# Hybrid streaming encoder step: the eight tiles of squares of a norm are added on GpSimd, and TensorE multiplies one tile by the averaging matrix

## The chip, the cores and the metric

The kernel runs on one core of one Trainium2 chip. The metric is the device time of one execution in microseconds; the number given for a kernel is the median of several executions. The engines are called by the names of the profile: PE (TensorE), ACT (ScalarE), DVE (VectorE), POOL (GpSimd) and SP (the queue of the transfers).

## The reference

Two layers of an encoder trunk work on 1024 prompt frames and 32 sample frames of width 1024, all in float32. Each layer normalizes its stream four times: before and after the mixer, and before and after the MLP.

```
def rms_norm(x, g):
    xf = x.astype(jnp.float32)
    r = lax.rsqrt(jnp.mean(xf * xf, axis=-1, keepdims=True) + EPS)
    return (xf * r).astype(x.dtype) * g
...
h = rms_norm(xp, g_pre_mix[l]) * (1 + sc1) + sh1
... two head groups of attention on project(h, w_in[l]) give o ...
xp = xp + gt1 * rms_norm(jnp.dot(o, w_out[l]), g_post_mix[l])
# mlp_sublayer
h = rms_norm(x, g_pre) * (1 + scale) + shift
u = jnp.square(jax.nn.relu(jnp.dot(h, w_up)))
return x + gate * rms_norm(jnp.dot(u, w_down), g_post)
```

The mean runs over the 1024 features of a frame. The change is about this mean alone.

## The kernel before

The activations lie transposed: features on the 128 partitions, in `KT` = 8 feature tiles, and the 1056 frames along the free dimension, cut into `NCH` = 3 chunks of `CH` = 352 frames. Products are formed from float32 operands that are split into a high and a low part (`hh`, `hl`, `wh`, `wl`, `uh`, `ul`), three matmuls for each product (lines 1522 to 1524).

A norm of one chunk passes over four engines. ACT squares all eight tiles of the chunk in one instruction into `sq` (`pre_sq`, line 611, and `post_sq`, line 630) and raises `sq_ok`. PE multiplies the eight tiles of `sq` by `onesd`, a 128x128 matrix filled with 1/1024, and accumulates them in one PSUM bank (`mean`, line 1552), so that every partition holds the mean of its frame. ACT turns the mean into the reciprocal root `rb` with a logarithm and an exponential (`norm_rb`, lines 603 and 605). DVE scales by it: `pre_scale` (line 1056) and `pre_lo` (line 1072) for a norm ahead of a projection, where ACT writes `hh` between the two (`pre_hi`, line 620); `post_rms` (line 1081) and `post_add` (line 1091) for a norm that goes back into the stream.

The four norms of a layer are called `NPRE1`, `NPOST1`, `NPRE2` and `NPOST2`. With three chunks and two layers there are 24 means. Every engine has its instructions in an order that is written out by hand, and each executes them strictly in that order; `npos` numbers the 24 means in this order. Around the entry to the MLP PE has this order: the groups `y` 0 to 11 of the output projection's second half (24 matmuls each, `q` is the group's number), with the mean of `NPOST1` chunk 0 behind group 4, of `NPRE2` chunk 0 behind group 7, of `NPOST1` chunk 1 behind group 8, and of `NPRE2` chunk 1 and `NPOST1` chunk 2 behind group 11; then the MLP's first step, with the mean of `NPRE2` chunk 2 behind its fourth group. Below these six are called m1 to m6. The same six stand, with `NPOST2` and the next layer's `NPRE1`, around the boundary between the two layers, behind shorter groups of 12 matmuls (1.9 us each). In the last step of the last layer there are three `NPOST2` means, the third of them at the very end.

The squares of a `NPRE` norm are those of the stream that the `NPOST` norm of the same chunk has just written. So a chain leads from m1 through ACT, DVE (`post_rms`, `post_add`), ACT (`pre_sq`) to m2, and from m2 through `pre_scale`, `pre_lo`, `post_rms` and `post_add` of the next chunk on DVE to the squares of m4.

POOL has only memsets, and copies and subtractions in the attention stage (lines 510 to 561); between these stages it is idle.

Of the kernel before, what the change touches and what calls it, by code (L numbers as in the profile page):

```python
# [15 lines left out]
ALU = mybir.AluOpType  # L16
# [8 lines left out]
KT = D // P  # L25
SEQ, NEW = 1024, 32
TOK = SEQ + NEW
NCH = 3
CH = TOK // NCH
# [3 lines left out]
DEPTH = 2  # L33
# [27 lines left out]
NPRE1, NPOST1, NPRE2, NPOST2 = range(4)  # L61
# [11 lines left out]
def build(nc, a):  # L73
    ctx = ExitStack()
    with ctx:
        base = 16512

        def at(name, shape, dt, off):
            return nc.alloc_sbuf_tensor_at(name, shape, dt, offset=base + off)

        def sem(name):
            return ctx.enter_context(nc.semaphore(name))
# [5 lines left out]
        sq = at("sq", [P, KT, TOK], F32, 0)  # L88
# [71 lines left out]
        def small(name, shape, dt):  # L160
            n = int(np.prod(shape[1:])) * (2 if dt == BF16 else 4)
            t = nc.alloc_sbuf_tensor_at(name, shape, dt, offset=base + cpos[0])
            cpos[0] += (n + 31) // 32 * 32
            assert base + cpos[0] <= 229344, (name, cpos[0])
            return t

        ident = small("ident", [P, P], F32)
        onesd = small("onesd", [P, P], F32)
# [39 lines left out]
        ps = nc.alloc_psum_tensor("ps", [P, 8, 512], F32)  # L208
# [11 lines left out]
        def sm(name):  # L220
            if name not in S:
                S[name] = sem(name)
            return S[name]

        def wait_apart(e, held, *waits):

            for name, v in (held, *waits):
                if isinstance(v, int):  # L230
                    if v > 0:
                        e.wait_ge(sm(name), v)
                else:
                    e.wait_ge(sm(name), v)
# [34 lines left out]
        def n_of(it):  # L269

            return it[1] if it[0] == "f" else N_FM + it[1]
# [16 lines left out]
        def npos(l, nu, c):  # L288

            if nu == NPRE1:  # L290
                return c if l == 0 else 12 * l - 2 + 2 * c
            if nu == NPOST2:
                return 12 * l + 9 + (2 * c if l + 1 < DEPTH else c)
            return 12 * l + 3 + 2 * c + (nu == NPRE2)

        def slot(l, n):

            return (l * NW + n) % 2
# [209 lines left out]
        @block.gpsimd  # L508
        def _(pool):
            pool.memset(scp[:, :, :], 0.0).then_inc(sm("scp_zero"), 1)  # L510
            pool.memset(zerob[:, :], 0.0).then_inc(sm("zero_ok"), 1)
            pool.memset(epst[:, :], EPS).then_inc(sm("eps_ok"), 1)
            for l in range(DEPTH):

                wait_apart(pool, ("zero_ok", 1), ("w_used", l * NW + W_WO0))
                pool.memset(svh[:, :, 64:128].bitcast(F32), 0.0).then_inc(sm("sz_ok"), 1)
                pool.memset(svl[:, :, 64:128].bitcast(F32), 0.0).then_inc(sm("sz_ok"), 1)

                wait_apart(pool, ("zero_ok", 1), ("so_lo", (l + 1) * 16))
                pool.memset(fvh[:, :, 64:128].bitcast(F32), 0.0)  # L520
                pool.memset(fvl[:, :, 64:128].bitcast(F32), 0.0).then_inc(sm("fz_ok"), 1)
                n = 1
                for h in range(2):
                    for stack, value in ((k2, 1.0), (q2, -1.0)):

                        wait_apart(pool, ("zero_ok", 1), ("fz_ok", l * 5 + n))
                        pool.memset(stack[h][64:68, :].bitcast(F32), value).then_inc(sm("fz_ok"), 1)
                        n += 1

                def stacks_own(t, h):  # L530

                    pr = l * 4 + t
                    r = slice(64 * h, 64 * h + 64)
                    if t or h:
                        pool.wait_ge(sm("fs_mm"), pr * 16 if h else pr * 16 - 8)
                    else:
                        pool.wait_ge(sm("so_lo"), (l + 1) * 16)
                    pool.tensor_copy(q1[h][r, :], qf[r, t, 0:SEQ]).then_inc(sm("fq_own"), 1)
                    if h == 0:
                        pool.tensor_copy(q2[h][r, :], qf[r, t, 0:SEQ]).then_inc(sm("fq_own"), 1)  # L540
                    pool.tensor_copy(k1[h][r, :], kf[r, t, 0:SEQ]).then_inc(sm("fq_own"), 1)

                def o_lo(t, b):

                    c0 = (512, 0)[b]
                    pool.wait_ge(sm("fo_hi"), (l * 4 + t) * 2 + b + 1)
                    pool.tensor_tensor(hl[:, t + 4, c0:c0 + 512], qf[:, t, c0:c0 + 512], hh[:, t + 4, c0:c0 + 512].bitcast(F32),
                                       ALU.subtract).then_inc(sm("fo_lo"), 1)

                stacks_own(0, 0)  # L550
                for t in range(4):
                    pool.wait_ge(sm("fz_ok"), 5 * (l + 1))
                    pool.wait_ge(sm("fo_lo"), l * 8 + max(0, 2 * t - 1))
                    stacks_own(t, 1)
                    pool.wait_ge(sm("fq_own"), l * 20 + 5 * t + 5)
                    if t:
                        o_lo(t - 1, 1)
                    if t < 3:
                        stacks_own(t + 1, 0)
                    o_lo(t, 0)  # L560
                o_lo(3, 1)


        @block.scalar
# [954 lines left out]
        def _(pe):  # L1519
            def three(out, w_hi, w_lo, m_hi, m_lo, k, nk, start=True, stop=True):  # L1520

                pe.matmul(out, w_hi, m_hi, start=start and k == 0, stop=False)  # L1522
                pe.matmul(out, w_hi, m_lo, start=False, stop=False)  # L1523
                return pe.matmul(out, w_lo, m_hi, start=False, stop=stop and k == nk - 1)  # L1524
# [4 lines left out]
            for i in range(TT + 1):  # L1529
                pe.wait_ge(sm(f"xrow_in{i % 8}"), 16 * (i // 8 + 1))  # L1530
                w = P if i < TT else NEW
                for hf in range(2):
# [3 lines left out]
                    for k in range(4):  # L1536
                        ins = pe.transpose(ps[:, q % 4, k * w:(k + 1) * w], xrow[i % 8][0:w, (4 * hf + k) * P:(4 * hf + k + 1) * P], ident[0:w, 0:w])
# [7 lines left out]
            def mean(l, nu, c):  # L1545

                idx = npos(l, nu, c)
                s = idx % 2
                pe.wait_ge(sm("sq_ok"), idx + 1)
                pe.wait_ge(sm("ln_ok"), max(0, idx - 1))  # L1550
                for k in range(KT):
                    ins = pe.matmul(ps[:, 4 + s, 0:CH], onesd[:, :], sq[:, k, c * CH:(c + 1) * CH], start=(k == 0), stop=(k == KT - 1))  # L1552
                ins.then_inc(sm("mean_ok"), 1)

            def modulate(out, halves):
# [8 lines left out]
            def mod_columns(out, rows):  # L1564

                pick = ident[:, :].rearrange("p (g n) -> p g n", g=4)[:, :, 0:2]
                return pe.matmul(out, rows, pick, start=True, stop=True, skip_group_check=True)

            for l in range(DEPTH):

                pe.wait_ge(sm("zero_ok"), 1)
                if l == 0:
# [9 lines left out]
                    for b in range(NB1):  # L1582
                        ins = mod_columns(ps[:, 6, 8 * b:8 * b + 8], mrow1[:, b * P:(b + 1) * P])
# [36 lines left out]
                for q, it in enumerate(PJ):  # L1620
                    b, n = q % 4, n_of(it)
# [12 lines left out]
                    if it[0] == "t":  # L1634
                        _, u, i = it
# [3 lines left out]
                        for k in range(KT):  # L1639
                            ins = three(ps[:, b, 0:w], hh[:, k, ts], hl[:, k, ts], whv[:, k, :], wlv[:, k, :], k, KT)  # L1640
                    else:
                        _, blk, j, c = it
                        cs = slice(c * CH, (c + 1) * CH)
                        if blk < 2:
                            pe.wait_ge(sm("h_ok"), l * 6 + c + 1)
                        for k in range(KT):
                            ins = three(ps[:, b, 0:CH], whv[:, k, j * P:(j + 1) * P], wlv[:, k, j * P:(j + 1) * P],
                                        hh[:, k, cs], hl[:, k, cs], k, KT)
# [173 lines left out]
                for b in range(NB2):  # L1822
                    ins = mod_columns(ps[:, 7, 8 * b:8 * b + 8], mrow[:, b * P:(b + 1) * P])
# [25 lines left out]
                for w in range(4):  # L1849
# [5 lines left out]
                    for hd in range(4):  # L1855
# [4 lines left out]
                        if w < 2:  # L1860
                            ins = pe.matmul(out, qn, kst[r, w, :], start=True, stop=True)
# [5 lines left out]
                        ins = pe.matmul(out[:, PAST:W], identb[0:NEW, 0:NEW], causb[0:NEW, 0:NEW], start=False, stop=True)  # L1867
                    ins.then_inc(sm("a_mm"), 1)
                for w in range(4):
# [4 lines left out]
                    for kb, c0 in enumerate(starts):  # L1874
                        ins = pe.transpose(ps[:, (2, 6)[w % 2], kb * P:(kb + 1) * P], ap[w][:, c0:c0 + P], ident[:, :])
# [3 lines left out]
                    for hd in range(4):  # L1879
# [3 lines left out]
                        if w < 2:  # L1883
                            pe.matmul(out, cvs[:, 64 * w:64 * w + 64], pt[:, 0, pc], start=True, stop=False)
                            ins = pe.matmul(out, vs_new[NEWP:P, 64 * w:64 * w + 64], pt[NEWP:P, 1, pc], start=False, stop=True)
                        else:
                            for kb in range(2):
                                pe.matmul(out, cvf[:, kb, h * HD:(h + 1) * HD], pt[:, kb, pc], start=(kb == 0), stop=False)
                            ins = pe.matmul(out, vf[NEWP:P, TT, h * HD:(h + 1) * HD], pt[NEWP:P, 2, pc], start=False, stop=True)
# [13 lines left out]
                for r in range(2):  # L1903
                    n0 = l * NW + W_WO0 + r * 2
                    for q in range(12):

                        b, j, c = (q // 6, (q // 3) % 2, q % 3) if r == 0 else ((q // 2) % 2, q % 2, q // 4)
# [3 lines left out]
                        for k in range(KT):  # L1911
                            ins = step(W_WO0 + b, ps[:, q % 4, 0:CH], b, j, slice(c * CH, (c + 1) * CH), k, KT, hh, hl)
# [86 lines left out]
            for i in range(TT + 1):  # L1999
                t0 = i * P if i < TT else TAIL  # L2000
                pe.wait_ge(sm("x_ready"), DEPTH * 6 + 1 + (t0 + P - 1) // CH)
                for hf in range(2):
# [3 lines left out]
                    for k in range(4):  # L2006
                        ins = pe.transpose(ps[:, q % 4, k * P:(k + 1) * P], xr[:, 4 * hf + k, t0:t0 + P], ident[:, :])  # L2007
# [63 lines left out]
```

## Time and profile before

| what | us |
|---|---|
| median of 3 runs | 3165.98 |
| lowest and highest of them | 3157.59 and 3182.37 |
| profiled execution, its own time | 3182.45 |
| its span, first to last instruction | 3180.7 |
| PE busy in it | 2973.7 |
| POOL busy in it | 82.9 |
| mean granted clock of PE, as a share of full speed | 0.938 |

The profile comes from one execution, which took 16.5 us more than the median of the three. Busy times of the engines lie beside each other; PE, with 93% of the span, is the one that is hardly ever idle.

### The profile page before, as it was taken

What the parts mean: (1) busy time and instruction counts of PE and PEld (TensorE: products, weight loads), DVE (VectorE), ACT (ScalarE), POOL (GpSimd) and SP (SyncE); (2) the same over time, 40 slices, a digit from 0 to 9 for tenths busy, and PEclk for the clock granted to TensorE, in tenths of its full rate; (3) what the DMA queues carried; (4) which work ended last, traced back from release to release, by engine and by line L of the source; (5) the groups of instructions that cost most, each with busy time, mean ns of one, the idle gap of its engine ahead of it and who ended that gap; (6) DMA issues with size and microseconds to landing.
All of it is one profiled execution on the core that took longest, in us unless ns stands there. A gap on an engine that the chain in (4) does not pass through costs nothing. (4 is left out here: it accounts for less than half of the span.)

```text
span 3180.7 us, 48146 instructions
## 1 busy us (share of the span) xinstructions
PE 2973.7 (93%) x19659; PEld 2757.7 (87%) x19675; DVE 1316.5 (41%) x2391; ACT 964.9 (30%) x1944; POOL 82.9 (3%) x79
## 2 busy tenths in 40 slices
PE   6998878889999999999999988788999999999998
PEld 5998657759899999999989966677699999999997
DVE  4114647721633333333361356476136333333334
ACT  5212436622511122111242144365133211111222
POOL 0000011100000000000000000111000000000000
PEclk8998679969999999999999978799699999999998
DMA  7111230013221111112211113101212111111121
GB/s 279 41 57 56 80 107 2 17 40 109 81 67 64 56 53 49 56 53 66 106 65 54 43 55 133 54 2 43 88 57 72 51 43 41 51 40 53 40 81 55
DMA packets 135345, 203.33 MB, mean 64 GB/s; under 512 B 8352, under 2 KB 90320, under 8 KB 134672
## 3 DMA queue, kind: packets, MB, share of 16 engines
q1 hardware_dynamic: 135200, 201.27, 18.4%
q8 instruction: 106, 1.74, 0.2%
q14 instruction: 39, 0.32, 0.0%
HBM read 170.45 MB, written 31.00 MB: 63 GB/s over the span
## 5 line engine op out<-in xcount | busy, mean ns | idle before, releaser
L1522 PE MATMUL ps<-hh,wh 128*128 128x352 f32 x2304 | 755.3, 328 | 13.7 <-DVE wl L1045 11.0
L1524 PE MATMUL ps<-hh,wl 128*128 128x352 f32 x2304 | 743.8, 323 | 0.0
L1523 PE MATMUL ps<-hl,wh 128*128 128x352 f32 x2304 | 742.3, 322 | 0.0
L1522 PE MATMUL ps<-uh,wh 128*128 128x352 f32 x1536 | 500.2, 326 | 4.1 <-DVE modn L1472 2.6
L1523 PE MATMUL ps<-ul,wh 128*128 128x352 f32 x1536 | 493.0, 321 | 0.0
L1524 PE MATMUL ps<-uh,wl 128*128 128x352 f32 x1536 | 492.9, 321 | 0.0
L1522 PEld LDWEIGHTS ps<-hh,wh 128*128 128x128 f32 x2304 | 435.2, 189 | 18.9 <-DVE wl L1045 11.0
L1523 PEld LDWEIGHTS ps<-hl,wh 128*128 128x128 f32 x2304 | 436.7, 190 | 1.3
L1524 PEld LDWEIGHTS ps<-hh,wl 128*128 128x128 f32 x2304 | 435.1, 189 | 0.0
L1045 DVE TENSOR_TENSOR wl<-raw,wh 128x2048 fp32r<-128x2048 f32 (+1 forms) x90 | 206.2, 2291 | 370.5 <-ACT wh L567 370.5
L567 ACT ACTIVATE wh<-raw 128x2048 fp32r<-128x2048 f32 (+1 forms) x90 | 172.0, 1911 | 580.8 <-PE ps L1899 580.8
L1485 DVE TENSOR_TENSOR y<-ps,y 128x352 f32<-128x352 f32 x336 | 173.3, 523 | 363.6 <-PE ps L1524 363.3
L1522 PEld LDWEIGHTS ps<-uh,wh 128*128 128x128 f32 x1536 | 288.7, 188 | 6.7 <-DVE ul L1451 4.0
L1523 PEld LDWEIGHTS ps<-ul,wh 128*128 128x128 f32 x1536 | 288.9, 188 | 0.5
L1524 PEld LDWEIGHTS ps<-uh,wl 128*128 128x128 f32 x1536 | 288.1, 188 | 0.0
L1446 DVE TENSOR_TENSOR u_t<-r_t 128x352 f32<-128x352 f32 x192 | 100.8, 525 | 436.6 <-ACT r_t L973 434.5
L973 ACT ACTIVATE r_t<-ps 128x352 f32<-128x352 f32 x192 | 89.0, 464 | 515.6 <-PE ps L1524 515.6
L1522 PE MATMUL ps<-wh,hh 128*128 128x256 f32 (+1 forms) x720 | 208.5, 290 | 0.0
L1523 PE MATMUL ps<-wl,hh 128*128 128x256 f32 (+1 forms) x720 | 204.2, 284 | 0.0
L1524 PE MATMUL ps<-wh,hl 128*128 128x256 f32 (+1 forms) x720 | 203.3, 282 | 0.0
L1522 PEld LDWEIGHTS ps<-wh,hh 128*128 128x128 f32 x720 | 136.5, 190 | 0.4 <-issue 0.4
L1524 PEld LDWEIGHTS ps<-wh,hl 128*128 128x128 f32 x720 | 136.8, 190 | 0.0
(250 smaller groups left out, 3960.4 us busy)
## 6 DMA issues: line engine op xcount, KB each, us to landing
ada_v<-w_ada SPq DMA_DIRECT2D x32, 1024.0 KB, 6.9
raw<-w_up SPq DMA_DIRECT2D x32, 1024.0 KB, 5.1
raw<-w_down SPq DMA_DIRECT2D x32, 1024.0 KB, 4.9
raw<-w_in SPq DMA_DIRECT2D x16, 1024.0 KB, 5.6
x_kept<-xr SPq DMA_DIRECT2D x6, 1408.0 KB, 9.4
xf<-x_kept SPq DMA_DIRECT2D x2, 4224.0 KB, 12.7
x_kept<-xf SPq DMA_DIRECT2D x6, 1408.0 KB, 5.5
xr<-x_kept SPq DMA_DIRECT2D x2, 4224.0 KB, 13.1
```

The source lines that it names most:

```text
L567: return act.activation(out, in_, ACT.Copy, **kw)
L973: act.activation(r_t[q % 2][:, :], ps[:, q % 4, 0:CH], ACT.Relu).then_inc(sm("u_relu"), 1)
L1045: dve.tensor_tensor(wl[slot(l, n)][:, 0:w], raw[slot(l, n)][:, 0:w], wh[slot(l, n)][:, 0:w].bitcast(F32), ALU.subtract).then_inc(sm("w_lo" ...
L1446: dve.tensor_tensor(u_t[q % 2][:, :], r_t[q % 2][:, :], r_t[q % 2][:, :], ALU.mult).then_inc(sm("u_sq"), 1)
L1485: dve.tensor_tensor(y[:, kt, cs], ps[:, DB[last][q], 0:CH], y[:, kt, cs], ALU.add).then_inc(sm("d_add"), 1)
L1522: pe.matmul(out, w_hi, m_hi, start=start and k == 0, stop=False)
L1523: pe.matmul(out, w_hi, m_lo, start=False, stop=False)
L1524: return pe.matmul(out, w_lo, m_hi, start=False, stop=stop and k == nk - 1)
```

## The change

For 20 of the 24 means POOL adds the eight tiles of squares in place by halves: four tiles to four, two to two, one to one, three instructions one behind the other. PE then multiplies only tile 0 of `sq` by the averaging matrix. PE waits for `sum_ok` from POOL where it waited for `sq_ok` from ACT. The function `summed` leaves four means as they were: the three of `NPRE1` in the first layer, and the last of all (`NPOST2`, chunk 2, last layer). POOL's new work stands behind its attention work of each layer, in the order of the means. Nothing changes on ACT and DVE.

```diff
+        def summed(l, nu, c):
+            if (l == 0 and nu == NPRE1) or (l + 1 == DEPTH and nu == NPOST2 and c == 2):
+                return None
+            return npos(l, nu, c) - NCH
...
+            def sum_squares(l, nu, c):
+                cs = slice(c * CH, (c + 1) * CH)
+                i = summed(l, nu, c)
+                pool.wait_ge(sm("sq_ok"), npos(l, nu, c) + 1)
+                for x, n in enumerate((4, 2, 1)):
+                    if x:
+                        pool.wait_ge(sm("sq_add"), 2 * i + x)
+                    pool.tensor_tensor(sq[:, 0:n, cs], sq[:, 0:n, cs], sq[:, n:2 * n, cs], ALU.add).then_inc(*((sm("sq_add"), 1) if n > 1 else (sm("sum_ok"), 1)))
...
                 o_lo(3, 1)
+                for c in range(NCH):
+                    sum_squares(l, NPOST1, c)
+                    sum_squares(l, NPRE2, c)
+                for c in range(NCH):
+                    if summed(l, NPOST2, c) is not None:
+                        sum_squares(l, NPOST2, c)
+                    if l + 1 < DEPTH:
+                        sum_squares(l + 1, NPRE1, c)
...
-                pe.wait_ge(sm("sq_ok"), idx + 1)
+                i = summed(l, nu, c)
+                if i is None:
+                    pe.wait_ge(sm("sq_ok"), idx + 1)
+                else:
+                    pe.wait_ge(sm("sum_ok"), i + 1)
                 pe.wait_ge(sm("ln_ok"), max(0, idx - 1))
-                for k in range(KT):
-                    ins = pe.matmul(ps[:, 4 + s, 0:CH], onesd[:, :], sq[:, k, c * CH:(c + 1) * CH], start=(k == 0), stop=(k == KT - 1))
+                nk = KT if i is None else 1
+                for k in range(nk):
+                    ins = pe.matmul(ps[:, 4 + s, 0:CH], onesd[:, :], sq[:, k, c * CH:(c + 1) * CH], start=(k == 0), stop=(k == nk - 1))
                 ins.then_inc(sm("mean_ok"), 1)
```

PE before, in the second layer, where m4 and m5 stand between the last group of the output projection (`hh`, `wh_72`, `wl_74`), the small matmul that frees a weight slot (line 1899), and the first group of the MLP:

```order
9034 L1524 MATMUL ps<-hh,wl_74 128x352
9035 L1899 MATMUL ps<-cb,zerob 128x32
9036 L1552 MATMUL ps<-sq,onesd 128x352 [waits ln_ok,sq_ok]
9037 L1552 MATMUL ps<-sq,onesd 128x352 x7
9038 L1552 MATMUL ps<-sq,onesd 128x352 [waits ln_ok,sq_ok]
9039 L1552 MATMUL ps<-sq,onesd 128x352 x7
9040 L1522 MATMUL ps<-hh,wh_71 128x352 [waits u_relu,h_ok,w_lo]
```

PE at the same place in the changed kernel, whose lines have moved down by 26 to 31:

```order
9017 L1550 MATMUL ps<-hh,wl_74 128x352
9018 L1930 MATMUL ps<-cb,zerob 128x32
9019 L1583 MATMUL ps<-sq,onesd 128x352 [waits ln_ok,sum_ok] x2
9020 L1548 MATMUL ps<-hh,wh_71 128x352 [waits u_relu,h_ok,w_lo]
9021 L1549 MATMUL ps<-hl,wh_71 128x352
```

Each mean is one matmul with a wait where it was eight, and m4 and m5 stand next to each other (x2). POOL, between its last subtraction of a layer's attention and the following sums, in the changed kernel:

```order
44 L564 TENSOR_TENSOR hl<-qf,hh 128x512 [waits fo_hi] x2
45 L528 TENSOR_TENSOR sq<-sq 128x4x352 [waits sq_ok]
46 L528 TENSOR_TENSOR sq<-sq 128x2x352 [waits sq_add]
47 L528 TENSOR_TENSOR sq<-sq 128x352 [waits sq_add]
48 L528 TENSOR_TENSOR sq<-sq 128x4x352 [waits sq_ok]
```

Behind the two subtractions there was nothing before until the next layer's memsets; now there are the sums, m1's in the second to the fourth row and m2's from the fifth.

## Rows read from the trace of the kernel before

**Rows 1.** Page, span and busy time of engines, share, instructions.

```profile
span 3180.7 us, 48146 instructions
...
PE 2973.7 (93%) x19659; PEld 2757.7 (87%) x19675; DVE 1316.5 (41%) x2391; ACT 964.9 (30%) x1944; POOL 82.9 (3%) x79
```

**Rows 2.** Busy time by stretch: the entry to the MLP, second layer.

```profile
2337.00:2412.00 75.00, 75.00 (x390) 64.58 (x389) 46.06 (x76) 39.30 (x51) 0.00 (x0) 1.00 0.24 84
```

**Rows 3.** Source view of line 1552: durations, and who waited for it.

```profile
L1552 PE MATMUL ps<-sq,onesd x384: 457/459/956, 22.2 to 3156.9; 128*128 128x352 f32 x192
...
ACT rb L603: 69.7, 20
```

**Rows 4.** Timeline of PE, line 1552: start, duration; second layer's m1 to m6.

```profile
2340.62 4.89 PE L1552 MATMUL ps<-sq,onesd 128*128 128x352 f32 x16
2356.87 4.90 PE L1552 MATMUL ps<-sq,onesd 128*128 128x352 f32 x16
2365.42 4.89 PE L1552 MATMUL ps<-sq,onesd 128*128 128x352 f32 x16
2381.88 9.71 PE L1552 MATMUL ps<-sq,onesd 128*128 128x352 f32 x32
2406.68 4.89 PE L1552 MATMUL ps<-sq,onesd 128*128 128x352 f32 x16
```

**Rows 5.** Timeline of ACT: the squares of m1 to m6.

```profile
2337.47 2.56 ACT L630 ACTIVATE sq<-y 128x2816 f32<-128x2816 f32 x1
...
2353.89 2.56 ACT L611 ACTIVATE sq<-xf 128x2816 f32<-128x2816 f32 x1 [0.20 <-DVE xf L1091]
...
2357.56 2.55 ACT L630 ACTIVATE sq<-y 128x2816 f32<-128x2816 f32 x1
...
2379.20 2.56 ACT L611 ACTIVATE sq<-xf 128x2816 f32<-128x2816 f32 x1 [0.55 <-DVE xf L1091]
...
2382.53 2.55 ACT L630 ACTIVATE sq<-y 128x2816 f32<-128x2816 f32 x1
...
2402.17 2.55 ACT L611 ACTIVATE sq<-xf 128x2816 f32<-128x2816 f32 x1
```

**Rows 6.** Timeline of DVE between m2 and the squares of m4.

```profile
2362.92 4.06 DVE L1056 SCALAR_TENSOR_TENSOR y<-xf,coef,rb 128x352 f32<-128x352 f32 x8 [9.07 <-ACT rb L605]
...
2372.00 3.08 DVE L1081 TENSOR_TENSOR y<-y,rb 128x2816 f32<-128x2816 f32 x1
```

**Rows 7.** Groups of POOL by line and form: busy, mean ns.

```profile
L547 POOL TENSOR_TENSOR hl<-qf,hh 128x512 fp32r<-128x512 f32 x16 | 20.4, 1276 | 262.6 <-ACT hh L567 262.6
...
L538 POOL CAST q1a<-qf 64x1024 fp32r<-64x1024 f32 x8 | 8.3, 1032 | 51.4 <-PE ps L1752 51.2
```

**Rows 8.** Timeline of POOL in the first layer's attention.

```profile
462.40 0.95 POOL L527 MEMSET k2a<- 4x1024 f32 x1
463.46 0.94 POOL L527 MEMSET q2a<- 4x1024 f32 x1
...
468.56 2.02 POOL L541 CAST k1a<-kf 64x1024 fp32r<-64x1024 f32 x1
```

**Rows 9.** Timeline of DVE in the same stretch.

```profile
467.66 2.02 DVE L1295 TENSOR_TENSOR q1a<-qf,q1a 64x1024 fp32r<-64x1024 f32 x1 [6.49 <-POOL q1a L538]
470.61 1.22 DVE L1298 TENSOR_TENSOR k2a<-kf,k1a 64x1024 fp32r<-64x1024 f32 x1 [0.93 <-POOL k1a L541]
```

**Rows 10.** Timeline of PE in a projection: a wait of 2.82 us.

```profile
243.62 0.46 PE L1595 MATMUL ps<-ident,ro 128*128 128x128 f32 x2 [2.82 <-DVE ro L1176]
```

**Rows 11.** Busy time by stretch behind that wait; the granted clock follows POOL's count.

```profile
244.65:248.06 3.41, 3.41 (x21) 3.41 (x20) 0.45 (x3) 0.00 (x0) 0.00 (x0) 0.61 0.00 0
248.06:251.48 3.42, 3.42 (x33) 3.42 (x31) 1.39 (x6) 0.38 (x1) 0.00 (x0) 1.00 0.03 7
```

**Rows 12.** Timeline of PE, line 1552, at the boundary between the layers.

```profile
1584.08 5.00 PE L1552 MATMUL ps<-sq,onesd 128*128 128x352 f32 x16 [1.06 <-ACT sq L611]
...
1610.70 9.73 PE L1552 MATMUL ps<-sq,onesd 128*128 128x352 f32 x32 [1.34 <-ACT sq L611]
```

## Prediction

> **What bounds the kernel now.** I read the page first: PE is busy for 2973.7 of 3180.7 us, POOL for 82.9 [rows 1]. That makes PE's work worth removing and POOL look free. But the change also puts POOL into a chain on which PE waits in order, so the shares decide nothing; the question is when the squares of a mean are ready and when PE comes to it. The busy time by stretch shows PE without a gap over the 75 us around the entry to the MLP [rows 2]. There PE's own work is the path, and only just, as the next two views show.
>
> The source view of line 1552 gives the size of a mean: a float32 matmul is two records, so 8 tiles are 16 records (384 for 24 means), each 459 ns long [rows 3]. The timeline shows the 16 of one mean lasting 4.89 us [rows 4], so they start (4.89 - 0.46) / 15 = 0.295 us apart. One tile is two records: 0.295 + 0.46 = 0.75 us. ACT waits for 20 of the means, 69.7 us in all [rows 3]: the mean is also latency for what follows.
>
> Then the slack, the end of the squares on ACT [rows 5] against the start of the mean on PE [rows 4]. m1: 2340.03 against 2340.62, 0.6 us. m2: 2356.45 against 2356.87, 0.4. m3: 2360.11 against 2365.42, 5.3. m4: 2381.76 against 2381.88, 0.1. m5: 2385.08 against 2386.7 (m4's start and half of 9.71), 1.7. m6: 2404.72 against 2406.68, 2.0. PE comes to its means almost as soon as they can run.
>
> **The change part by part.** *Removed:* 14 of 16 records of 20 means, 14 x 0.295 = 4.14 us each, 83 us of PE's time in all.
>
> *Added:* a POOL sum between the squares and the mean. The trace has no such add; the nearest row is POOL's two-input subtraction over 512 columns, 1.276 us [rows 7], 2.49 ns a column. The three adds have 1408 + 704 + 352 = 2464 columns. In proportion they take 6.1 us; with some 0.1 us of each instruction fixed, (1.276 - 0.1) / 512 = 2.3 ns a column and 5.7 + 0.3 = 6.0. I take 6.0. From one POOL instruction to one that waits for it lie 463.46 - 462.40 - 0.95 = 0.11 us [rows 8], twice; the hand-overs from ACT and to PE I estimate at 0.05 each. So **a sum makes a mean ready 6.3 us behind the end of its squares**, and a second sum that is queued in POOL 6.2 us behind the first.
>
> The Trainium skill (GPSIMD Engine Reference, section 3.1) gives 4497 ns for such an add over 2048 columns. By that the sum of 2464 columns would be an estimated 5.4 us and ready at 5.8; this case's row is longer a column (2.49 ns against 2.2), and it decides.
>
> A lone mean with slack s then moves PE by 6.3 - s - 4.14 us. It loses where s is under 2.2, and m1, m2, m4, m5 and m6 all lie there. I walk the second layer's entry, each number a shift against before:
> - m1: 6.3 - 0.6 - 4.14 = +1.6. What follows from it moves with it: `rb`, DVE, the squares of m2.
> - m2: again 6.3 - 0.4 - 4.14 = +1.7, together +3.3. PE has only 3 groups of some 3.9 us between m1 and m2, and comes to m2 nearly 6 us early.
> - m3: POOL starts its sum when m2's is done, so it is ready 6.2 us behind, while PE needs 0.75 + 3.9. PE waits 1.6 and saves 4.14. This one gains, but it leads nothing: DVE goes from m2 straight through `pre_scale`, `pre_lo` and `post_rms` [rows 6], whose last begins at 2372.0, directly behind `pre_lo`.
> - m4: its squares come from that DVE chain, +3.3, and the sum puts its start at 3.3 + 6.3 - 0.1 = +9.5; its end, with 4.14 saved, at +5.3. m3's gain is gone.
> - m5: its squares are ready during m4's sum, so it ends 6.2 + 0.75 = 6.95 behind m4's start, where it was 9.71: 9.5 + 6.95 - 9.7 = **+6.7**.
> - m6: its squares end 13.1 us behind the end of m5 (2404.72 - 2391.59), then 6.3 + 0.75 make 20.2; it was 2411.57 - 2391.59 = 20.0. So +6.9, and the MLP behind it is PE's own pace again.
>
> So +7 us for an entry, with 6 means and 25 us of PE's work removed. The first layer has the same hand-written order: +7. At the boundary PE already waits for squares, 1.06 us ahead of the second mean and 1.34 ahead of the fourth [rows 12], so the slack there is nil: +1.6 for the first as for m1, 6.3 - 4.14 = +2.1 for the second and the fourth, and the queued fifth and the sixth as in the entry, in all some +6. In the last step two lone means stand behind groups of PE as m1 does, +1.6 each: +3. **Bare walk: 7 + 7 + 6 + 3 = +23 us.**
>
> *What POOL and DVE do to each other.* In the attention stage a POOL cast takes 2.02 us beside a DVE operation with two operands in SBUF [rows 8, 9] where it takes 1.03 otherwise [rows 7], and the DVE operation 2.02 where its like, over as many columns, takes 1.22 [rows 9]. Each gives the other some 0.9 us. In the walk the sum of m3 runs beside `pre_scale` (4.06 us on the chain), that of m5 beside a weight split, `pre_scale` and `post_rms`, that of m6 beside the MLP's squares. From below this costs nothing (DVE waits only for what ends soon); from above DVE stands through the rest of one add and two more, about 4 us, and POOL through 3 us of DVE's work at m5. I take 5 of 7 us for an entry, 4 for the boundary, nothing at the end, where DVE's adds read PSUM: 5 + 5 + 4 = **+14 us**.
>
> The Trainium skill (SBUF — State Buffer, section "Who interferes with whom") says that such a pair holds a shared port in turn, the second one blocked until the first is done. By that the upper value would hold, 7 + 7 + 6 = 20 instead of 14. The row fits a block of one instruction's length as well as a sharing, so it settles nothing, and I stay at 14.
>
> *What PE's waiting does to its clock.* Behind a PE wait of 2.82 us [rows 10] the granted clock fell from 1.0 to a mean of 0.61 over the next 3.4 us, the half level, 1.2 GHz, for most of them, and 21 matmuls ran where 33 run in the stretch behind [rows 11]. That is 12/33 x 3.41 = 1.2 us lost there, and 1.5 with the end of the stretch ahead of it. The new waits of PE are 5.7 us at m1, 5.9 at m2, 6 to 8 at m4, over 5 at m5. Where PE comes early to the next mean anyway (between m1 and m2, and m2 and m4) the loss is hidden in that wait. It shows behind m6, and in part between m5 and m6. Bounds: nothing, or 1.5 at each of the 17 waits (26 us). I take 3 for each entry, 2 for the boundary, 1.5 for each of the last two means, behind which PE's work is the path: **+11 us**.
>
> Sum: 23 + 14 + 11 = **+48 us**, against the profiled execution's 3182.5 that is 3230. Against the median of the three runs, from which the comparison is made, 3166 + 48 = **3214 us**, +1.5%.
>
> **The rivals.** (a) *The bare walk:* the clock's loss hides in the next wait everywhere and POOL and DVE step aside cheaply. +23, 3189 us. For it: most of DVE's time in these stretches is waiting. Against: rows 8 to 11 show both effects in this kernel, the clock's after a wait half as long.
>
> (b) *The whole price:* a mean is ready 6.6 us behind its squares and not 6.3 (+5 over the walk), POOL and DVE cost each other 20, and the clock 1.5 at each of 17 waits: 23 + 5 + 20 + 26 = +74, 3240 us.
>
> (c) *POOL adds fast*, the rival on the other side: at the cast's pace, 1.03 us for 1024 columns [rows 7], the adds take 2.5 us and a mean is ready 2.9 us behind its squares, for reasons such as that `fp32r` output or other shapes make the subtraction slow. A lone mean then gains 4.14 + 0.5 - 2.9 = 1.7. The walk of an entry gives -1.7, -3.4, -4.8 at m4, -6.3 at m5, -9.5 at m6; twice that, 9 for the boundary and 3.4 for the end are -31: 3135 us. It decides where the sum is ready within 4.14 + 0.5 = 4.6 us. Against it: two inputs instead of one, and both rows of POOL scale with what it reads.
>
> (d) *The adds are hidden*, and all 83 us come back: 3083 us. It would need slack of over 6 us at each mean; one of six has 5.3.
>
> **How the numbers follow.** The chances: forecast 0.58, within 3198 to 3232; (a) 0.22; (b) 0.12; (c) 0.06; (d) 0.02. The median of three moves by some 10 us from run to run (3157.6 to 3182.4), and 1%, 32 us, is about what a measurement can tell. Slower by over 1% is above 3197.7: nearly all of the forecast (0.54) and (b), 0.66. Within 1%: (a), the rest of the forecast and half of (c), 0.29. Faster: 0.05. The range takes in (a) with room below for a sum ready at 5.8, and (b): 3176 to 3243.
>
> **What the changed profile would show.** Three POOL adds at about 3.4, 1.7 and 0.9 us each in a quiet stretch, longer beside DVE; POOL's busy time up by 20 x 6 = 120 us or more. PE waiting for POOL 17 to 20 times, 5 to 8 us each, about 90 us in all, and PE busy 83 us less but for the slow clock. The distance from m1 to m6 some 5 us longer in the bare walk, 13 to 15 with the rest. Short stretches at half clock around 2345 to 2420, where none was. The middle steps of the MLP and the attention unchanged.
>
> Wrong would be: adds under 4 us in sum (c), no clock dips (a), or squares that come earlier relative to PE than before, because some group of PE's work ahead of them grew.

## The result, and the profile after

The changed kernel takes 3218.8 us (median of 4 runs, 3216.2 to 3225.5) against 3163.6 for the kernel before (4 runs, 3157.6 to 3182.4). The ratio is 1.017 with a 95% interval of 1.0145 to 1.0195: 46 to 62 us slower. The forecast was +48 us and 3214. One execution of the last but one kernel below took 4134 us at a mean granted clock of 0.64; the comparisons leave it out.

The page of the changed kernel, its span and busy times:

```profile
span 3219.0 us, 47646 instructions
...
PE 2910.1 (90%) x19379; PEld 2718.8 (84%) x19395; DVE 1343.3 (42%) x2391; ACT 965.3 (30%) x1944; POOL 210.9 (7%) x139
```

PE has 280 records and 64 us of busy time less than in [rows 1], and the kernel is slower. POOL has 128 us more, which the share of 7% makes look harmless. The waits of PE, from the view of who waited for whom (total us, times, longest), have a new first line:

```profile
PE ps L1583 <- POOL sq L528: 104.5, 17, 11.9
```

These are 17 waits, the number for which the prediction counted the clock's price. PE waits 104.5 us in exchange for 83 us of removed work. The timeline of PE shows the waits at the second entry to the MLP, where [rows 4] had no idle time (m1, m2, m4, m5, m6; m3 did not have to wait):

```profile
2363.46 1.54 PE L1583 MATMUL ps<-sq,onesd 128*128 128x352 f32 x2 [5.28 <-POOL sq L528]
2382.69 1.54 PE L1583 MATMUL ps<-sq,onesd 128*128 128x352 f32 x2 [5.16 <-POOL sq L528]
2413.74 1.54 PE L1583 MATMUL ps<-sq,onesd 128*128 128x352 f32 x2 [11.87 <-POOL sq L528]
2419.92 1.54 PE L1583 MATMUL ps<-sq,onesd 128*128 128x352 f32 x2 [4.64 <-POOL sq L528]
2442.34 1.54 PE L1583 MATMUL ps<-sq,onesd 128*128 128x352 f32 x2 [3.95 <-POOL sq L528]
```

Each mean takes 1.54 us for its two records and not 0.75: it runs while the granted clock is at the half level, behind PE's wait. The timeline of POOL in the same stretch (x3 is one sum, x6 two in a row):

```profile
2357.51 5.90 POOL L528 TENSOR_TENSOR sq<-sq 128x1408 f32<-128x1408 f32 x3 [121.26 <-ACT sq L656]
2376.70 12.19 POOL L528 TENSOR_TENSOR sq<-sq 128x1408 f32<-128x1408 f32 x6 [13.29 <-ACT sq L637]
2405.84 14.03 POOL L528 TENSOR_TENSOR sq<-sq 128x1408 f32<-128x1408 f32 x6 [16.94 <-ACT sq L637]
2434.35 7.93 POOL L528 TENSOR_TENSOR sq<-sq 128x1408 f32<-128x1408 f32 x3 [14.48 <-ACT sq L637]
```

A sum by itself takes 5.9 us, hand-overs between its adds included; m1 starts 2363.46 - 2357.43 = 6.0 us behind the end of its squares (6.3 forecast). The sums of m4 and of m6 lie beside DVE's work and take 2 us more each; m5's, queued behind m4's, takes 6.2 us. POOL's groups by form give the adds as 3.5, 1.7 and 1.2 us on average; those of m1 take 3.16, 1.67 and 0.93 us. DVE, beside the second sum of a pair, in its own timeline (4.06 us in [rows 6]):

```profile
2385.39 6.38 DVE L1082 SCALAR_TENSOR_TENSOR y<-xf,coef,rb 128x352 f32<-128x352 f32 x8 [12.04 <-ACT rb L631]
```

Single instructions show how the two meet. The timelines of POOL and DVE in two narrow windows, at m4's last add (0.93 us in a quiet stretch) beside a weight split of DVE (2.3 us otherwise), and at m3's second add (1.67 us) beside the second of the eight instructions of `pre_scale` (0.58 us):

```profile
2410.83 2.86 POOL L528 TENSOR_TENSOR sq<-sq 128x352 f32<-128x352 f32 x1
2410.53 2.38 DVE L1071 TENSOR_TENSOR wl<-raw,wh 128x2048 fp32r<-128x2048 f32 x1 [5.15 <-ACT wh L593]
...
2385.86 1.85 POOL L528 TENSOR_TENSOR sq<-sq 128x704 f32<-128x704 f32 x1
2386.08 2.01 DVE L1082 SCALAR_TENSOR_TENSOR y<-xf,coef,rb 128x352 f32<-128x352 f32 x1
```

The one that started first runs at nearly its own pace (2.38 and 1.85 us), and the other ends some 0.4 to 0.8 us behind it. They take turns; they do not slow each other down evenly.

And the busy time by stretch, with the granted clock behind POOL's count; the first is the whole entry, the second m4 and m5:

```profile
2354.00:2441.00 87.00, 57.44 (x303) 53.47 (x301) 53.65 (x74) 38.86 (x50) 37.91 (x17) 0.80 0.20 70
2405.00:2426.00 21.00, 7.62 (x24) 6.08 (x25) 12.29 (x12) 10.98 (x16) 13.72 (x6) 0.52 0.16 59
```

The kernel before had 1.00 there [rows 2].

**Where the time is.** The two profiled executions differ by 38 us in span, the medians by 55. To see why, both are cut at the squares of m1 of a stretch (ACT's timeline) and at the memset that ends the projection (POOL's timeline). The kernel before:

```profile
777.59 2.56 ACT L630 ACTIVATE sq<-y 128x2816 f32<-128x2816 f32 x1
1563.62 2.56 ACT L630 ACTIVATE sq<-y 128x2816 f32<-128x2816 f32 x1 [13.61 <-DVE y L1485]
1861.89 0.53 POOL L516 MEMSET svh<- 128x512 f32 x1 [1202.98 <-PE ps L1654]
3106.61 2.56 ACT L630 ACTIVATE sq<-y 128x2816 f32<-128x2816 f32 x1 [13.45 <-DVE y L1485]
```

The changed kernel, with the start of its second entry as the fourth row:

```profile
770.82 2.56 ACT L656 ACTIVATE sq<-y 128x2816 f32<-128x2816 f32 x1
1572.90 2.56 ACT L656 ACTIVATE sq<-y 128x2816 f32<-128x2816 f32 x1 [13.58 <-DVE y L1511]
1888.16 0.53 POOL L533 MEMSET svh<- 128x512 f32 x1 [225.76 <-PE ps L1685]
2354.87 2.56 ACT L656 ACTIVATE sq<-y 128x2816 f32<-128x2816 f32 x1
3139.71 2.56 ACT L656 ACTIVATE sq<-y 128x2816 f32<-128x2816 f32 x1 [13.46 <-DVE y L1511]
```

In the kernel before, the second entry starts at 2337.47 [rows 5]. This gives the four stretches that hold all the changed means: first entry with its MLP (to the boundary), boundary with the projection, second entry with its MLP, and the last step to the end of the span. All kernels below are cut in the same way; "four together" is the sum of the rounded entries, and "comparison" is the ratio to the kernel before, with its interval, from the timed runs. The stretches come from one execution of each kernel; the two entries, which do the same work, shift by the same amount within 0.6 us in every kernel.

| kernel | entry 1 | boundary | entry 2 | end | four together | against before | comparison |
|---|---|---|---|---|---|---|---|
| before | 786.0 | 298.3 | 769.1 | 74.1 | 1927.5 | | |
| changed | 802.1 | 315.3 | 784.8 | 79.3 | 1981.5 | +54.0 | 1.0170 (1.0145 to 1.0195) |
| one tile, no sum | 773.4 | 286.6 | 756.5 | 64.0 | 1880.5 | -47.0 | 0.9872 (0.9848 to 0.9895) |
| filled waits | 799.3 | 311.8 | 782.1 | 75.5 | 1968.7 | +41.2 | 1.0157 (1.0137 to 1.0177) |
| half sum | 793.0 | 301.6 | 775.6 | 71.9 | 1942.1 | +14.6 | 1.0056 (1.0034 to 1.0078) |
| lone sums | 800.8 | 313.0 | 783.8 | 81.1 | 1978.7 | +51.2 | 1.0166 (1.0146 to 1.0187) |
| lone sums, filled | 794.2 | 304.0 | 777.4 | 75.8 | 1951.4 | +23.9 | 1.0102 (1.0069 to 1.0134) |
| sum where slack | 789.4 | 301.5 | 772.3 | 74.2 | 1937.4 | +9.9 | 1.0041 (1.0019 to 1.0063) |
| fp32r mean | 774.2 | 285.7 | 757.3 | 62.6 | 1879.8 | -47.7 | 0.9863 (0.9830 to 0.9896) |

The changed kernel has +16.1, +17.0, +15.7 and +5.2 us in the four, 54.0 together, and the comparison says +54. What lies outside them is 1253.2 us in the profiled execution before and 1237.5 in the one after; the last section says where that comes from. None of the changed means lies there.

### The profile page after: what moved, and what is told of

The parts are those of the page before. It is cut to its first block and busy times, and to the rows that moved or that the text cites. A ratio compares the mean times of both kernels' runs of the same rounds, so it can differ in the third digit from the quotient of the medians.

```text
span 3219.0 us, 47646 instructions
## 1 busy us (share of the span) xinstructions
PE 2910.1 (90%) x19379; PEld 2718.8 (84%) x19395; DVE 1343.3 (42%) x2391; ACT 965.3 (30%) x1944; POOL 210.9 (7%) x139
## 5 line engine op out<-in xcount | busy, mean ns | idle before, releaser
L1548 PE MATMUL ps<-hh,wh 128*128 128x352 f32 x2304 | 763.8, 332 | 13.5 <-DVE wl L1071 11.0
L1472 DVE TENSOR_TENSOR u_t<-r_t 128x352 f32<-128x352 f32 x192 | 107.5, 560 | 436.7 <-ACT r_t L999 434.6
L528 POOL TENSOR_TENSOR sq<-sq 128x1408 f32<-128x1408 f32 (+2 forms) x60 | 127.9, 2135 | 1817.7 <-ACT sq L656 1677.2
L1583 PE MATMUL ps<-sq,onesd 128*128 128x352 f32 x104 | 50.7, 628 | 111.0 <-POOL sq L528 104.5
```

Source lines behind the costliest of these rows:

```text
L528: pool.tensor_tensor(sq[:, 0:n, cs], sq[:, 0:n, cs], sq[:, n:2 * n, cs], ALU.add).then_inc(*((sm("sq_add"), 1) if n > 1 else (sm("sum_ok") ...
L1472: dve.tensor_tensor(u_t[q % 2][:, :], r_t[q % 2][:, :], r_t[q % 2][:, :], ALU.mult).then_inc(sm("u_sq"), 1)
```

## The experiments

### The removal alone: one tile, no sum

The squares of seven of the eight tiles are left out of the mean in this kernel, so its results are not the reference's.

```diff
-                if i is None:
-                    pe.wait_ge(sm("sq_ok"), idx + 1)
-                else:
-                    pe.wait_ge(sm("sum_ok"), i + 1)
+                pe.wait_ge(sm("sq_ok"), idx + 1)
...
-                    sum_squares(l, NPOST1, c)
-                    sum_squares(l, NPRE2, c)
...
```

> POOL's sums are left out and PE multiplies only tile 0 of the squares, as soon as ACT has written them, so the mean is that of the first 128 features and the results differ from the reference. What is left is the removal alone. If PE's own work is the whole path, all 20 x 4.14 = 83 us come off the kernel before: about 3081 us. By my walk the gain is smaller, because the squares of m4 come from the DVE chain behind m2 and m3's share is lost in a wait: five of six in an entry, 20 us each for the two entries and the boundary, 8 at the end, about 68 us off: 3095 us. If the chain through ACT and DVE were the path and PE's work lay beside it, the gain would be near 0.

Measured: 3123.8 us against 3168.8, ratio 0.987 (0.985 to 0.990); the four stretches are 47.0 us shorter. So of 83 us of PE's work only 47 could be had even by an add that costs nothing, and my walk, with 68, was too good as well. The waits and the timeline of PE, and ACT's timeline behind it, show where the rest is; the PE row is m4's:

```profile
PE ps L1572 <- ACT sq L629: 21.3, 8, 5.4
...
2339.15 1.54 PE L1572 MATMUL ps<-sq,onesd 128*128 128x352 f32 x2 [5.37 <-ACT sq L629]
...
2339.49 2.55 ACT L648 ACTIVATE sq<-y 128x2816 f32<-128x2816 f32 x1
2341.94 1.90 ACT L585 ACTIVATE wh<-raw 128x2048 fp32r<-128x2048 f32 x1
2343.74 0.54 ACT L621 ACTIVATE rb<-ps,epst 128x352 f32<-128x352 f32 x1
```

PE waits for the squares of m4 as the walk has it. But it also gains nothing between m4 and m6: from m4's squares to m6's are 22.6 us in this kernel (2336.55 to 2359.14 in ACT's timeline) and 23.0 before [rows 5]. ACT makes the squares of m5 and a weight split ahead of m4's `rb` in its hand-written order, and DVE has a split, `pre_scale`, `post_rms` and `post_add` behind it. The chain through ACT and DVE stands close behind PE in these stretches. PE's own waits also bring the half clock on here (m4 takes 1.54 us); no run takes that away from this kernel, so how much of the missing 36 us is the clock stays open.

### PE kept busy in its waits: filled waits

```diff
                 else:
+                    last_step = nu == NPOST2 or (nu == NPRE1 and c < 2)
+                    for _ in range({NPOST1: (34, 0, 30), NPRE2: (34, 72, 24), NPOST2: (34, 0, 30), NPRE1: (34, 60, 12)}[nu][c] if not (l + 1 == DEPTH and nu == NPOST2) else 34):
+                        pe.matmul(ps[:, 0 if last_step else 7, 0:CH], zerob[:, :], cb[:, 0:CH], start=True, stop=True)
                     pe.wait_ge(sm("sum_ok"), i + 1)
```

> The changed kernel, with dummy bf16 matmuls of 352 columns (0.15 us each) into an unused PSUM bank ahead of each wait for a sum: 34 at a lone mean (5 us), 60 to 72 at m4 (9 to 11 us), 30 at m5, 12 to 24 at m6, none at m3. They end before the sum is ready or close to it, so PE is busy where it was idle, and nothing else changes. Theory (the clock is a term of its own, 11 us in the prediction): the half clock vanishes from these stretches and 5 to 15 us come back, 3204 to 3214 us. Rival (the clock's loss hides in the next wait everywhere): 3219 us or a little more, with the half clock gone from the trace all the same.

Measured: 3218.0 us, ratio 1.0157 (1.0137 to 1.0177). The times alone do not tell this kernel from the changed one (3218.8 us). The trace does. Busy time by stretch over the second entry:

```profile
2364.00:2450.00 86.00, 79.43 (x494) 66.10 (x492) 55.78 (x75) 38.83 (x50) 38.72 (x18) 1.00 0.21 75
```

The clock is 1.00 where it was 0.80, and the four stretches are 12.8 us shorter than the changed kernel's (2.8, 3.5, 2.7 and 3.8). What lies outside them is 15.9 us longer: 1253.4 us of this execution against 1237.5, nearly all of it in the two attention stages of the last section. The medians are nearly equal, so if the four stretches repeat from one execution to the next, some 12 us are lost outside in them as well; why this kernel meets the longer stages that often is not shown. The clock's term is thus seen in the trace of one execution and not in the medians; the last run with dummy matmuls gives a second sight of it. At m3 PE now waits, in its timeline:

```profile
2397.24 0.86 PE L1586 MATMUL ps<-sq,onesd 128*128 128x352 f32 x2 [1.60 <-POOL sq L528]
```

### A smaller sum: half sum

```diff
-                for x, n in enumerate((4, 2, 1)):
-                    if x:
-                        pool.wait_ge(sm("sq_add"), 2 * i + x)
-                    pool.tensor_tensor(sq[:, 0:n, cs], sq[:, 0:n, cs], sq[:, n:2 * n, cs], ALU.add).then_inc(...)
+                pool.tensor_tensor(sq[:, 0:4, cs], sq[:, 0:4, cs], sq[:, 4:8, cs], ALU.add).then_inc(sm("sum_ok"), 1)
...
-                nk = KT if i is None else 1
+                nk = KT if i is None else 4
```

> POOL makes only the first of the three adds (four tiles to four), PE multiplies the four tiles that hold the sums. A lone mean is ready 3.4 us behind its squares instead of 6.1, and PE saves 8 of 16 records, 2.36 us. By the walk a lone mean costs 3.4 - 0.5 - 2.36 = +0.6 instead of +1.6 against the kernel before, m4's chain 3 x that, m5's is no longer queued: about +3 for an entry instead of +7, in all +9, plus port and clock at well under half of their price (waits of 3 us): 3164 + 15 = 3179 us, between 3170 and 3190. A rival in which the number of waits counts and not their length would leave it near 3219.

Measured: 3183.7 us, ratio 1.0056 (1.0034 to 1.0078), the four stretches +14.6, as expected. PE waits for POOL 14 times, 50.7 us in all. The number of waits has fallen little, from 17; their sum has halved and the loss is a quarter. That fits a loss that is set by how far a sum's latency exceeds the slack and the saved time together, and not by how many waits there are.

### The queued sums taken out: lone sums

```diff
+        def lone(l, nu, c):
+            return c >= 1 and nu in (NPOST1, NPOST2) and not (l + 1 == DEPTH and nu == NPOST2)
...
+            if lone(l, nu, c):
+                return None
-            return npos(l, nu, c) - NCH
+            return LONE.index(npos(l, nu, c))
```

`LONE` holds the means that keep their sum, in order; those of which `lone` is true (m3, m5 and their like) are multiplied from eight tiles again.

> The changed kernel, but the means whose sums are queued in POOL behind another (m3 and m5 of each entry, and their like at the boundary, six in all) are multiplied from eight tiles by PE again, without a sum. These are the sums that lie beside pre_scale and post_rms on DVE. By the walk m5 ends 4.73 instead of 6.95 us behind m4's start, so 2 us of each of three stretches come back, and m3 costs nothing more, because PE waits at m4 anyway. If the port is the term that I gave it (14 us), most of it comes back too: 3219 - 6 - 12 = about 3201 us. Rival (the port costs little): 3213 us. Rival (PE's work is what counts, 6 x 4.14 more of it): 3244 us.

Measured: 3219.9 us, ratio 1.0166 (1.0146 to 1.0187); the four stretches are 2.8 us under the changed kernel. This is none of my three numbers. `pre_scale` is back to 4.06 us, but `pre_lo` behind it waits, in DVE's timeline; ACT's timeline shows what for:

```profile
2383.98 4.06 DVE L1091 SCALAR_TENSOR_TENSOR y<-xf,coef,rb 128x352 f32<-128x352 f32 x8 [12.23 <-ACT rb L640]
2390.74 4.06 DVE L1107 SCALAR_TENSOR_TENSOR hl<-y,mod,hh 128x352 fp32r<-128x352 f32 x8 [2.70 <-ACT hh L655]
...
2388.32 0.47 ACT L602 ACTIVATE y<-ps 128x352 f32<-128x352 f32 x1 [4.38 <-PE ps L1559]
2388.68 3.94 ACT L655 ACTIVATE hh<-y,mod 128x352 fp32r<-128x352 f32 x8
```

`pre_lo` in the kernel before, DVE's timeline:

```profile
2368.02 4.06 DVE L1072 SCALAR_TENSOR_TENSOR hl<-y,mod,hh 128x352 fp32r<-128x352 f32 x8 [1.04 <-ACT hh L620]
```

ACT's `hh` is late because ACT first has to fetch PE's group 8, and the first half of that group ran at half clock behind the wait for m2: the group takes 6.2 us, where 3.9 is its time at full clock. What DVE got back from POOL, the clock took. That is a reading of the rows; the next run puts it to the test.

### Both taken out: lone sums, filled

The edit is the last one, and the dummy matmuls of the filled run ahead of the remaining waits.

```diff
+                    for _ in range({NPOST1: (34, 0, 0), NPRE2: (34, 50, 30), NPOST2: (34, 0, 0), NPRE1: (34, 44, 24)}[nu][c] if not (l + 1 == DEPTH and nu == NPOST2) else 34):
+                        pe.matmul(ps[:, 0 if last_step else 7, 0:CH], zerob[:, :], cb[:, 0:CH], start=True, stop=True)
```

> The run with lone sums, with the dummy matmuls ahead of each wait for a sum as in the filled run (34 at a lone mean, 50 at m4 and 44 at its like, 24 to 30 at m6; none at the means without a sum). With lone sums alone nothing came back, and its trace shows why it may be: the group behind m2 and m3's eight tiles ran at half clock, ACT waited for that group ahead of its hh, and DVE waited for hh. If the port and the clock each cost what they seem to and stand in for each other, taking away both gives back more than the two alone: by the bare walk with lone sums +5 for an entry and the boundary and +3 at the end, 3165 + 20 to 25 = 3188 us, up to 3195. If the port costs nothing, only the clock's 8 to 12 us come off the lone sums: 3208 us. If neither counts, 3218.

Measured: 3196.2 us against 3163.4, ratio 1.010 (1.007 to 1.013); the four stretches +23.9. The timelines of POOL, DVE and PE at the second entry:

```profile
2361.32 5.95 POOL L536 TENSOR_TENSOR sq<-sq 128x1408 f32<-128x1408 f32 x3 [11.93 <-ACT sq L646]
2388.27 5.95 POOL L536 TENSOR_TENSOR sq<-sq 128x1408 f32<-128x1408 f32 x3 [20.99 <-ACT sq L646]
2414.12 7.90 POOL L536 TENSOR_TENSOR sq<-sq 128x1408 f32<-128x1408 f32 x3 [19.90 <-ACT sq L646]
...
2369.35 4.06 DVE L1091 SCALAR_TENSOR_TENSOR y<-xf,coef,rb 128x352 f32<-128x352 f32 x8 [10.69 <-ACT rb L640]
2374.45 4.05 DVE L1107 SCALAR_TENSOR_TENSOR hl<-y,mod,hh 128x352 fp32r<-128x352 f32 x8 [1.04 <-ACT hh L655]
...
2388.30 7.62 PE L1590 MATMUL ps<-cb,zerob 128*128 128x352 bf16 x50
```

Without the half clock the wait for `hh` is 1.04 us, as in the kernel before; the DVE row of the lone sums had 2.70. Taking out the queued sums gives 2.8 us back at the slow clock (54.0 to 51.2) and 17.3 at the full one (41.2 to 23.9); filling the waits gives 12.8 with the queued sums in place and 27.3 without (51.2 to 23.9). The medians agree here in the main: 3219.9 to 3196.2 is 24 us, and the two ratios differ by 20. The kernel has a flaw of its own: the 50 dummy matmuls ahead of m4 are too many. They last until 2395.9, m4's sum is done at 2394.2, and its mean starts 1.5 us late, in both entries. Some 3 of the 23.9 us come from that, and 17.3 and 27.3 are too low by as much. So both are causes, and each hides the other.

### A sum only where there is slack

```diff
-            return c >= 1 and nu in (NPOST1, NPOST2) and not (l + 1 == DEPTH and nu == NPOST2)
+            return not (c == 1 and (nu == NPOST1 or (nu == NPOST2 and l + 1 < DEPTH)))
```

> Sums on POOL for three means only, m3 of each entry and its like at the boundary, which have 5 us of slack; the other 21 are as in the kernel before. By the walk PE waits 1 us and saves 4.14 at each, and loses it again in the wait for the squares of m4, which come from DVE's chain behind m2: no gain, 3165 us. The sum lies beside pre_scale, which stands on that chain, and costs it about 2 us each: 3165 + 6 = 3171 us at most. If PE's work is what counts, 3165 - 3 x 3.1 = 3156 us.

Measured: 3181.7 us against 3163.4, ratio 1.0041 (1.0019 to 1.0063), +6 to +20 us; the four stretches +9.9. No gain, as the walk has it, and more of a loss than I gave it. The timelines of POOL, DVE and PE:

```profile
2355.95 6.30 POOL L536 TENSOR_TENSOR sq<-sq 128x1408 f32<-128x1408 f32 x3 [141.34 <-ACT sq L666]
...
2358.68 6.44 DVE L1092 SCALAR_TENSOR_TENSOR y<-xf,coef,rb 128x352 f32<-128x352 f32 x8 [9.06 <-ACT rb L641]
...
2379.03 11.43 PE L1593 MATMUL ps<-sq,onesd 128*128 128x352 f32 x32 [4.15 <-ACT sq L647]
```

The sum is nearly hidden (PE waits 1 us for it at m3), but `pre_scale` beside it takes 6.44 instead of 4.06 us on the chain that leads to m4. What PE saves at m3 it waits at m4, 4.15 us, and behind that wait its clock is at the half level for part of the time: m4 and m5 take 11.43 us where they took 9.71 [rows 4]. One sum with slack costs 3.3 us.

### A cheaper mean on PE: fp32r

The experiments say that a mean may become shorter, but not later. The matmuls of the mean are float32, two records each; in the kernel before they are put into fp32r, one record each, like those of the projections.

```diff
-        sq = at("sq", [P, KT, TOK], F32, 0)
+        sq = at("sq", [P, KT, TOK], F32R, 0)
...
+        onesr = at("onesr", [P, P], F32R, mt + 9728)
...
+            dve.tensor_copy(onesr[:, :], onesd[:, :])
...
-                    ins = pe.matmul(ps[:, 4 + s, 0:CH], onesd[:, :], sq[:, k, c * CH:(c + 1) * CH], start=(k == 0), stop=(k == KT - 1))
+                    ins = pe.matmul(ps[:, 4 + s, 0:CH], onesr[:, :], sq[:, k, c * CH:(c + 1) * CH], start=(k == 0), stop=(k == KT - 1))
```

`onesr` lies where the attention stage has a value tile, so DVE copies it anew ahead of each entry.

> The kernel before, with the squares and the averaging matrix in fp32r: each of the eight matmuls of a mean is one record with a start-to-start of 0.16 us, as those of the projections, where it was two with 0.295 each. No sum on POOL, no new wait. A mean takes some 1.3 us instead of 4.73, 3.4 us less at all 24. The squares are rounded to fp32r, which the average over 1024 of them should hardly show. If the gain follows the run with one tile and no sum, where 83 us of removed work gave 45 back, 20 x 3.4 = 68 give 37, and the last mean 3 more: 3129 us, about 40 under the kernel before. If the one-tile run's lost 38 us came from something other than the chain through ACT and DVE (which this kernel shares), the gain would be 70 or more.

Measured: 3127.7 us against 3163.4, ratio 0.986 (0.983 to 0.990); the four stretches -47.7. The kernel is faster than the kernel before and than the changed one. The timeline of PE (m1 and m4 of the second entry):

```profile
2313.49 1.45 PE L1555 MATMUL ps<-sq,onesr 128*128 128x352 f32 x8
...
2348.44 2.72 PE L1555 MATMUL ps<-sq,onesr 128*128 128x352 f32 x8 [3.96 <-ACT sq L612]
```

1.45 us where it was 4.89. It stops at the same barrier as one tile without a sum: m4 waits 3.96 us for its squares and then runs at the half clock. In the four stretches the one kernel has 83 us less of PE's work and this one 21 x 3.44 = 72, and both are 47 to 48 us shorter. That points to the rest of the chain as the limit.

## Why the prediction was right

**The bounding view.** PE was the path only by 0.1 to 2.0 us at five of six means, and the slack between squares and mean told it. There are 17 waits, all but m3's and its like. The walk has a wait of 1.6 us at m3 too, and it is missing for a reason that the walk left out: the group ahead of m3 ran in part at the half clock, and PE came to m3 0.5 us behind its sum. In the filled kernel, at full clock, the wait is there, 1.60 us. The waits are 2.3 to 11.9 us long and 104.5 us together, where I had 5 to 8 and about 90.

**The price of a sum.** 6.0 us for three adds, measured 5.8 (3.16 + 1.67 + 0.93) and 5.9 with the hand-overs between them; 6.3 to the mean, measured 6.0. The row of a 512-column subtraction carried over in proportion. By the figure of the Trainium skill (GPSIMD Engine Reference, section 3.1) for the same kind of add the estimate was 5.4 us for the adds and 5.8 to the mean. The trace lies between the two.

**The bare walk, 23 us.** The filled kernel shows it best, because its clock is up and its dummy matmuls end in time. m2 ends 3.0 us later against the squares of m1 than in the kernel before (3.3 in the walk). An entry costs 13.1 us, of which 6.4 belong to POOL and DVE by the next paragraph: 6.7 are left, where I had 7. In the same way the boundary has 7 (6 forecast; 0.7 us of half clock at its m5, which the dummy matmuls do not remove, is taken off), and the last step 1.4 (3 forecast), some 22 us in all.

**POOL and DVE in each other's way, 14 us: the term that was too small.** In an entry of the filled kernel `pre_scale` makes the squares of m4 2.1 us later, m4's last add waits 1.9 us for a weight split, the squares of m6 lose 0.4, and m6's adds lose 2.0 beside the squares of the MLP: 6.4 us, where I had 5 and an upper value of 7. At the boundary the places are `pre_scale` (2.3), m5's first add (2.0) and m6's (1.2). Together that is an estimate of 18 us. I had put the loss at m5's sum in the entry; it is m4's. The Trainium skill (SBUF — State Buffer, section "Who interferes with whom") has DVE and POOL hold a port in turn and block each other for whole instructions. The rows agree: m4's add of 0.93 us took 2.86 beside a DVE instruction that itself took 2.38 instead of 2.3. I stayed at 14 because rows 8 and 9 fitted a sharing as well; by whole blocks I had 20, and 18 is closer to that. For the lone sums I had expected 12 us of this and 6 of the queue, which is part of the walk; they gave 17.3 at full clock, or up to 20 with the flaw of that run taken off.

**The clock, 11 us.** 12.8 us in the trace of the filled kernel, 27.3 with the queued sums away, and 20 to 24 of these in the timed runs. The size was right and the reason only in part. I held that the loss hides between m1 and m4 because PE comes early there. PE does; but ACT takes PE's groups in order, so a group at half clock delays the squares of m3 and `hh` behind it, and through them DVE. The loss of the clock travels through ACT's queue.

**The sum, and where luck helped.** In this order the terms are 22, 18 and 13 us, where I had 23, 14 and 11. By stretch I had 15 for an entry, 12 for the boundary and 6 for the end, and they came to 16, 17 and 5: most of what was missing is at the boundary. That each term comes out near its forecast depends on the order in which they are taken away. Taken last, with the queued sums gone, the clock is worth more than twice as much. I had added the terms as if they were independent, and they are not.

**What I had wrong without harm.** The gain that a free add would bring, 68 us by the walk, is 47: the step "m5 ends behind m4's start" counts PE's time alone, and ACT's own order (squares of m5, a weight split, then m4's `rb`) sets it when PE gets faster. In the changed kernel, where PE gets slower, this did not show.

**The rivals.** The bare walk alone (+23) falls by the table: clock, queue and port are there, 30 us of 54. The whole price (+74) was too much. The fast add falls by POOL's 5.9 us. The hidden add falls twice: by the 17 waits, and because even the free one gives 47 of 83.

## What to carry to other kernels

Before work is moved from a busy engine to an idle one, read the slack at the place where the result comes back: here 2.6 us or less at 17 of 20 places, against 6 us of added latency and 4 us of saved work, and the shares of busy time (93% and 3%) said the opposite. The sum in the three places with 5 to 6 us of slack still cost 3.3 us each. If the work is shortened where it stands (the same matmul in fp32r, 1.45 instead of 4.89 us) there is no hand-over to pay for. And if two suspects can hide each other, take both away in one run: each alone gave 3 and 13 us back, both together 30.

## What the runs showed of the hardware

In the changed kernel the granted clock fell around each of PE's waits of 5 us at m1 and m2, to 1.2 GHz for 6.8 us, and at m4 and m5, with waits of 11.9 and 4.6 us, to a mean of 0.52 over 21 us.

A two-input add on POOL took 3.16, 1.67 and 0.93 us for 1408, 704 and 352 columns. Beside two-input instructions of DVE the two engines took turns by whole instructions, as the rows of the result show.

The time outside of the four stretches moves by up to 19 us between the profiled executions (1234 to 1253 us), though the instructions there are the same in all kernels but the last. Most of it sits in the attention stage with the sliding window, which took 159.7 us in the first layer before and 153.2 after, and 158.6 and 151.0 in the second: 14 of the 16 us between these two. One such stage in the kernel before, the changed one and the half sum, by busy time and clock:

```profile
1861.80:2020.60 158.80, 129.44 (x1016) 99.17 (x1014) 93.76 (x171) 72.77 (x229) 1.08 (x3) 0.73 0.31 109
...
1888.10:2039.20 151.10, 121.60 (x1016) 93.31 (x1014) 93.70 (x171) 72.85 (x229) 1.03 (x3) 0.79 0.33 114
...
1863.50:2012.20 148.70, 119.15 (x1016) 90.95 (x1014) 93.54 (x171) 72.78 (x229) 1.12 (x3) 0.80 0.34 116
```

1016 records of PE each, DVE and ACT alike, and the granted clock at 0.73, 0.79 and 0.80: PE waits and works by turns there, and the share that falls to the half level differs; what decides it is not shown. Differences of under 10 us between medians of this kernel, and of some 12 for the filled one, may be nothing else, and cutting the trace at landmarks tells more than the span does.
